# A hybrid attention, retention and MLP block on eight cores: rows split at 2272, meta tokens inside the first full chunk, 32 leftover rows in array strips, merge sums on VectorE

## What is computed

```python
h = concat([meta, x])                              # 16 + 4096 rows per sequence
proj = rmsnorm(h) @ w_in                           # q,k,v of attention; q,k,v,gate of retention; two gates
s = einsum('qd,kd->qk', rope(q), rope(k)) * scale  # 4 heads, two maps each, causal
a = softmax(s1) - lam * softmax(s2);  oa = rmsnorm(a @ v)
# retention: per 128-row chunk, with a state R carried from chunk to chunk
o = (q @ k.T * decay) @ v + (q @ R) * xi;   R = c * R + k.T @ (v * zeta)
merged = sigmoid(g_a) * (oa @ w_pa) + sigmoid(g_r) * (norm(o) * silu(r_g) @ w_pr)
h = h + merged @ w_o
h = h + square(relu(rmsnorm(h) @ w_up)) @ w_down
out = rmsnorm(h)[16:]
```

## Time and profile before

| | us |
|---|---|
| median of 3 runs (lowest, highest) | 4253.72 (4249.52, 4260.27) |
| the profiled execution | 4252.16 |
| its span, slowest core (2) | 4250.4 |
| cores of role a (0, 2, 4, 6) | 4241.9, 4250.4, 4239.1, 4240.2 |
| cores of role b (1, 3, 5, 7) | 4149.8, 4149.6, 4147.7, 4137.9 |
| core 2: PE, weight loads, DVE, ACT, POOL busy | 4180.3, 2321.0, 1619.4, 878.6, 559.4 |

### The profile page before, as it was taken

The page is one execution under the profiler, slowest core; times in us unless marked ns, Lnnn a source line. Parts: engine busy times, 40 slices in busy tenths (PEclk is TensorE's granted clock), DMA queues, the critical chain, the costliest instruction groups (busy, mean ns, idle before and its releaser), DMA issues.

```text
span 4250.4 us, 68858 instructions; the slowest of 8 cores (4137.9 to 4250.4 us)
## 1 busy us (share of the span) xinstructions
PE 4180.3 (98%) x24090; PEld 2321.0 (55%) x24228; DVE 1619.4 (38%) x2909; ACT 878.6 (21%) x2214; POOL 559.4 (13%) x1039
## 2 busy tenths in 40 slices
PE   8999999999999999999999999999999999999998
PEld 6565565555555566665445555555555555555554
DVE  5265477767741111111333223333234333222334
ACT  3020355655631111111111110001112000111002
POOL 1000122222222222121000000000001000000000
PEclk9999999999999999999999999999999999999999
DMA  8544767677769665576777444444459444444442
GB/s 215 145 138 112 156 132 169 151 151 155 155 145 202 172 172 137 138 178 173 247 243 200 68 70 67 68 70 66 69 96 261 70 69 66 70 70 68 68 68 97
DMA packets 381145, 549.03 MB, mean 129 GB/s; under 512 B 223233, under 2 KB 302721, under 8 KB 363009
## 3 DMA queue, kind: packets, MB, share of 16 engines
q0 software_dynamic: 77904, 197.23, 30.0%
q1 hardware_dynamic: 302898, 347.34, 28.2%
HBM read 597.89 MB, written 100.14 MB: 164 GB/s over the span
## 4 chain that ended last, share of the span: by engine, by line
PE 92%; DMA 4%; issue 1%; DVE 1%; ACT 1%; POOL 0%; SPq 0%; POOLq 0%; DVEq 0%; ACTq 0%
PE ps L438 91%; DMA sb_a_w_1_0_134_194<-w 1%; DMA sb_a_w_1_2_136_196<-w 1%; DMA sb_a_w_1_3_137_197<-w 1%; DMA sb_a_xf_12_72<-xin 1%; PE ps L681 0%; PE ps L469 0%; DMA sb_a_aT_69_129<-sb_a_P_65_125 0%; DMA sb_a_r_1_133_193<-or_d_a 0%; SPq L273 0%; ACT sb_a_P_67_127 L1303 0%; DMA sb_a_aT_70_130<-sb_a_P_65_125 0%; PE ps L1113 0%; DMA V_d_a<-sb_a_vs_44_104 0%; DMA sb_a_aT_70_130<-sb_a_P_66_126 0%
## 5 line engine op out<-in xcount | busy, mean ns | idle before, releaser
L1735 ACT ACTIVATE sb_a_rl_170_230<-ps 128x384 f32<-128x384 f32 x192 | 94.2, 491 | 1270.4 <-PE ps L438 1259.2
L1735 ACT ACTIVATE sb_a_rl_171_231<-ps 128x384 f32<-128x384 f32 x192 | 94.3, 491 | 403.7 <-PE ps L438 403.7
L438 PE MATMUL ps<-sb_a_wR_116,sb_a_xR_57_117 128*128 128x512 bf16 x606 | 151.7, 379 | 0.1
L438 PE MATMUL ps<-sb_a_wR_116,sb_a_xR_60_120 128*128 128x512 bf16 x605 | 150.0, 379 | 0.1
L438 PE MATMUL ps<-sb_a_xR_57_117,sb_a_wR_116 128*128 128x384 bf16 x768 | 148.8, 329 | 0.0
L438 PE MATMUL ps<-sb_a_xR_60_120,sb_a_wR_116 128*128 128x384 bf16 x768 | 147.6, 329 | 0.0
L1303 ACT ACTIVATE sb_a_P_67_127<-ps 128x464 bf16<-128x464 f32 (+15 forms) x216 | 110.1, 510 | 109.0 <-PE ps L438 85.3
L438 PEld LDWEIGHTS ps<-sb_a_xR_60_120,sb_a_wR_116 128*128 128x128 bf16 x768 | 74.0, 99 | 44.1 <-issue 2.8
L438 PEld LDWEIGHTS ps<-sb_a_xR_57_117,sb_a_wR_116 128*128 128x128 bf16 x768 | 73.4, 99 | 43.3 <-issue 2.5
L1489 DVE SCALAR_TENSOR_TENSOR sb_a_m_125_185<-sb_a_tg_121_181,ps 128x384 f32<-128x384 f32 x48 | 26.6, 554 | 173.8 <-PE ps L438 105.5
L438 PEld LDWEIGHTS ps<-sb_a_wR_116,sb_a_xR_60_120 128*128 128x128 bf16 x608 | 57.5, 98 | 54.7
(11 more groups left out here) (704 smaller groups left out, 9298.1 us busy)
## 6 DMA issues: line engine op xcount, KB each, us to landing
sb_a_xR_60_120<-xnT_d_a SPq DMA_DIRECT2D x24, 768.0 KB, 5.8
...
sb_a_x_1_131_191<-xnT_d_a SPq DMA_DIRECT2D x11, 1536.0 KB, 9.7
sb_a_wb_156_216<-w_up POOLq DMA_DIRECT2D x22, 512.0 KB, 5.6
sb_a_wb_157_217<-w_up POOLq DMA_DIRECT2D x22, 512.0 KB, 5.8
sb_a_wb_158_218<-w_up POOLq DMA_DIRECT2D x22, 512.0 KB, 5.5
sb_a_wb_159_219<-w_up POOLq DMA_DIRECT2D x22, 512.0 KB, 5.5
```

Of the source, the lines that this page charges most:

```text
L438: ins = h.matmul(out_ap, l, r, start=(start and i == 0), stop=(stop and i == n - 1), skip_group_check=loose)
L1735: p.act(lambda e, r=r, bk=bk, n=n: e.activation(out=rl[r][:, 0:n], in_=PS[bk][:, 0:n], func=AF.Relu), writes=[PB[bk], B_rl[r]])
```

## The change

The border between the two cores moves from row 2304 to row 2272, so a owns 32 rows fewer and b 32 more.

- **Core a**: no prefix. Its first chunk now holds 16 zero rows, the 16 meta rows and the first 96 real rows; 18 chunks as before, all own. The first 32 rows are dropped behind the attention: tile 0 has 352 rows in stage 3 and in the up products of the first MLP pass; the chunk's 96 rows still fill one turn of weights in stage 4 and in the down products. Each attention unit has 32 keys and one key block fewer. The first chunk's retention has no state to read.
- **Core b**: 18 prefix chunks (six full tiles) instead of 19, 14 full own chunks and a last one of 32 rows (`TAIL`). Its last own tile has 288 rows instead of 256. Where the 32 rows are moving columns (keys and queries, stage 3, up products: 416 instead of 384 columns in the second pass) they lengthen the matmuls; where they are the weights, new matmuls with 32 output partitions are added: values, retention values and gate, four attention units.
- **Strips**: in stage 4 and the down products the 32 rows go through `mm_strips`: four matmuls in turn, with the same 32 rows as weights and four different blocks of 512 output columns, each writing its own 32 partitions of one PSUM bank. The four column blocks then lie under one another; `fold` adds the four partial sums of squares with a 128x128 f32 matrix.
- In the second MLP pass on b the four down weights of a block are refilled only behind its strips, instead of one after each 512 columns.
- **Merge sums** (`mo`) go from POOL to DVE, on both cores.
- On a, `o1` has two buffers instead of one.

```diff
+TAIL = 32
+ZERO = TAIL - 16
...
-        for c, n in even(nown, 9):
+        for c, n in even(nown - (1 if npre else 0), 9):
...
+    def rows(self, ch):
+        return TAIL if self.tail and ch == self.nch - 1 else 128
+    def own_rows(self, j):
+        lo = self.skip if j == 0 else 0
+        return lo, self.tt(self.n0 + j) - lo
...
-            return [(Z + a, w) for a, w in even(128 * (ch + 1) - Z, 512)]
+            return [(Z + a, w) for a, w in even(keys(ch) - Z, 512)]
...
-            p.pool(lambda e: e.tensor_tensor(out=mo[ms][:, fb, 0:n], in0=m12[f2][:, 0:n], in1=m12[f2 + 1][:, 0:n], op=ALU.add),
+            p.dve(lambda e: e.tensor_tensor(out=mo[ms][:, fb, 0:n], in0=m12[f2][:, 0:n], in1=m12[f2 + 1][:, 0:n], op=ALU.add),
...
+    def mm_strips(self, bk, pairs, reads):
+        PS = self.PS
+        def fn(h):
+            ins = None
+            for i, q in enumerate(pairs):
+                for s in range(4):
+                    ins = h.matmul(PS[bk][TAIL * s:TAIL * (s + 1), :], q[s][0], q[s][1], start=(i == 0), stop=(i == len(pairs) - 1), skip_group_check=True)
+            return ins
+        self.p.pe(fn, reads, [self.PB[bk]])
...
+                    self.mm_strips(4, [[(mt[:, kc, off:off + r], self.wo[q][0][:, kc, :]) for q in range(4)] for kc in range(16)],
+                                   [B_mt] + [b for _, b in self.wo])
...
+                def down_tail():
+                    ws = [(w0 + nb) % self.nwb for nb in range(4)]
+                    wv = [self.wb[s][:].rearrange("p (k f) -> p k f", k=8) for s in ws]
...
+                    self.mm_strips(bk, [[(u[f][:, t0:t0 + TAIL], wv[q][:, f, :]) for q in range(4)] for f in range(8)],
...
-                        self.wb_load()
+                        if not tail:
+                            self.wb_load()
+                    if tail:
+                        down_tail()
+                        for _ in range(4):
+                            self.wb_load()
...
-                    Core(nc, io, 1, SPLIT[0], "a", st).build()
+                Core(nc, io, 0, SPLIT[0], "a", st).build()
...
-                    Core(nc, io, 1 + SPLIT[0], SPLIT[1], "b", st).build()
+                Core(nc, io, SPLIT[0], SPLIT[1] + 1, "b", st).build()
```

More of the change, by code:

```diff
@@ L1110, in tfn @@
                     ins = None
-                    for cc in range(nchk):
+                    for cc in range(nt):
                         for b in range(2):
@@ L1207, in phase2 @@
         load_tile(0, 0)
-        load_tt(0)
-        if npre > 1:
-            load_tt(1)
+        for ch in range(min(npre, 2)):
+            load_tt(ch)
         queue += proj_steps(0)
@@ L1374, in slot @@
             if 0 <= u - 1 < NU:
-                n = 128 * (units[u - 1][1] + 1)
-                js = even(n - Z, 512)
+                js = even(keys(units[u - 1][1]) - Z, 512)
                 S.append((0.0, 0.0, lambda: ratio(u - 1)))
```

395 lines of the change are left out of this document (249 added, 146 removed).

## The result

The median of the changed kernel is **4202.39 us** (four runs, 4197.45 to 4207.76). Against the kernel before its ratio is **0.988, 95% interval 0.985 to 0.990**: 1.2% faster, clear of the noise, with the time predicted at 4222 (4184 to 4268). The profiled execution took 4207.76 us. (Now and then the four cores of one half of the chip run part of an execution at half the clock, whatever the kernel; only cores and stretches without that are compared here.)

What follows compares the result with a forecast made beforehand. TensorE bounds the kernel, core a ending before the change and b after it. For b, 4149.8 + 34.9 (matmuls) + 19.2 (strips) + 20 (width changes) - 5 (stage 3) = 4218.9, plus 3.4 gives 4222 us; range 4184 to 4268.

Steps and rivals of the forecast that it cites:

- Which core ends: Spans of both roles: b becomes later than a by some 33 us, 4218.9 against 4185.4.
- rival 3: Core a sets the end: b comes to 4187 and a, at 4189, is as late; chance 0.12.
- The counts: Matmuls removed or added on TensorE, priced at 0.416 ns a column plus 2.1 ns fixed; a loses 65.0 us.
- I count nothing: Core a, stage 2: the second o1 buffer may free a few us of idle time, entered as nothing.
- hidden on a: Merge sums on DVE, 0.56 us a block instead of 1.0 on POOL, fit within stage 3 blocks of 7.8 us.
- The strips: Core b, stages 4 and 5: 80 rounds of four matmuls at 0.24 us each, 19.2 us (17.2 to 69).
- Rival 1: Core b's strips run one after another, 0.86 us a round, time 4272; chance 0.14.
- rival 2: Some 320 32-row matmuls outside the strips lose their loads' cover: 84 us in place of 20, time 4286; chance 0.08.
- the 29 that were named as a refutation: Core b, stage 5: growth above 13.6 + 64 x 0.24 = 29 us would show the prediction wrong.
- Changes of width, 20: Core b: 242 switches between 32 and 128 output partitions, at most 0.164 us each; half of 0 to 40 us taken.
- Stage 3 on b, -5: Core b's m12 waits, 34 us, go; weights landing at 2393 bind next; stage 5 us shorter (-15 to +10).
- The sum: Core b's span: 4149.8 + 34.9 + 19.2 + 20 - 5 = 4218.9 us; with 3.4 added, a time of 4222.

Runs made afterwards that it cites:

- experiment 6: Changed kernel, even cores' chunks in tiles of 1, 3, 3, 3, 3, 3, 2 instead of six of 3: their stage 2 took 750.9 and 752.8 us.
- experiment 2: Changed kernel with core b's 32-row chunk's matmuls in stage 2 written 128 output partitions wide instead of 32: ratio to the kernel before 0.986.

## Why the prediction was right, and where it was off

- **Which core ends.** Right: b is the later one, by 38 us in the means of four executions (33 foretold). That the even cores stay slowest, the first thing that would have refuted it, did not happen, and rival 3 falls.
- **The counts.** Right to a microsecond wherever the stage is full: stage 1 on both roles, a's stage 5 (-13.6), and the price by columns of stage 2, -25.0 on a (25.8 foretold) and +24.4 on b (25.5).
- **Core a, "I count nothing"** for idle time. Right for the buffer it was said of, but the term itself was too small: 16 us came in stage 2, at most 6 of them matmuls at half the clock and the others waits, and 7.5 in stage 3. For stage 2 experiment 6 points to the tile of one chunk without measuring its share: the waits at its start were in the trace, with 0.60 of the clock, and the sum went by matmuls alone. The 7.5 go with the merge sums, which the prediction had put down as hidden on a: with them back on POOL a's stage 3 is 761 again, 8 below the kernel before, where 10 were counted for columns. It cost the prediction nothing, as a does not end.
- **The strips.** Right; 0.216 us a round, the lower bound, in place of 0.24. The 0.24 was drawn from the pace of short matmuls in order; starts 0.003 us apart show that strips are not held to that pace. Rival 1 falls, and rival 2 too, as narrow matmuls in a row have no such gap (median 0.010 us over the price, core 1's stage 2). Stage 5 on b grew by 31.2, more than the 29 that were named as a refutation: of the 31.2, 13.6 are columns, 13.8 strips, 1.6 the 16 changes of width (which that bound left out), 1.2 one wait at the new `fold`, and 1 is not placed. The bound was drawn without these small terms; the reason behind it stands.
- **Changes of width, 20.** The size came out right, 0.10 us each and 18.9 us in stage 2, but by luck: half of the upper bound was taken "for want of a nearer row". That the term adds to the time was half wrong: the last two columns of the table, waits and half-clock steps, shrank by 11.1 us in the same stage, and experiment 2 shows that more than half of the changes' time is waited elsewhere when they are gone. The 72 more exponentials cost nothing that shows. The rule of the Trainium skill (TensorEngine Tiling (Array Packing), Tiling Modes), that a change of mode drains TensorE, gets no clear answer: a change costs 0.094 to 0.109 us, not the 0.164 of a whole emptying, and as long as the load that starts only with its matmul there. Whether the engine drains or the load just loses its cover no run here tells apart.
- **Stage 3 on b, -5.** Mechanism right (no m12 waits, weights next), size off by 8 us: with the columns' +10.2 taken out the stage lost 23 us, not 15. The sum let the stage end with the last weights, and these hardly moved: counted from the stage's first matmul, the last piece of `w3` landed after 542 us before and after, the last of `wo` after 684 and 681 (means of the odd cores), while the stage ended after 681 and 668. The wrong step is that stage 4 would start with the last `wo` piece. The landing at 2392.7 in the earlier trace rows is the last but one; the last came at 2398.2, behind the start of stage 4 at 2395.2, whose first matmuls read another piece of `wo`, landed by 2301.6. Before the change they waited for m12. The wait for the last pieces now stands inside stage 4, on three of the four cores (core 3):

```profile
PE ps L466 <- DMA sb_b_wo_141_43335<-wo: 4.1, 1, 4.1
```

  Stage 4 has 6.6 us more where 3.8 were counted, so 3 of the 8 us came back there.
- **The sum.** 4218.9 for b's span: 4203.9 was read on core 1, 4202.5 in the mean of the profiled execution. Of the 16.4 between the sum and this mean, 10 are stage 2, 7.8 stage 3 and 3.5 core 1's distance from its role's mean before; the other stages take 5 off. The median lies 5 below the profiled execution, where 1.6 above it was taken.
